# Running gate sums broadcast by DMA instead of transposed, GpSimd's rotation behind two additions, two attention steps moved, the last norm's weights on ScalarE

## What is computed

```python
# first layer: gated delta rule, 8 q/k heads, 16 value heads, chunks of 64 in the reference
g = -exp(a_log) * softplus(aa + dt_bias)
g = cumsum(g over the chunk)                        # running gate sums
diff = g[..., :, None] - g[..., None, :]
decay = exp(where(causal, diff, -inf))
a_strict = where(strict, beta[..., :, None] * kk * decay, 0)
sol = triangular_solve(a_strict, rhs, unit_diagonal=True)
qk = einsum(q, k) * decay
# beside it: 8 heads of dilated attention, with a rotation of the first 32 columns
q_b = partial_rope(bq, pos); k_b = partial_rope(bk, pos)
y = concatenate([y_a, y_b]) @ w_out
# ... other layers ...
return x * rsqrt(mean(x * x) + eps) * norm_final_g  # last norm
```

## Time and profile before

| | us |
|---|---|
| median of 3 runs | 2892.57 (2891.11 to 2893.55) |
| the profiled execution | 2890.94 |
| its span, first to last instruction | 2889.2 |

### The profile page before, as it was taken

One profiled execution on the slowest core, in us unless ns is written; L12 is line 12 of the kernel. 1 busy time (PEld: TensorE's weight loads), 2 busy tenths in 40 slices (PEclk: granted clock), 3 DMA queues, 4 the chain that ended last, 5 costly groups with the idle time before them and its releaser, 6 DMA issues.

```text
span 2889.2 us, 51927 instructions
## 1 busy us (share of the span) xinstructions
PE 2839.9 (98%) x17818; PEld 2521.2 (87%) x17818; DVE 2143.4 (74%) x3130; ACT 1484.7 (51%) x2140; POOL 452.5 (16%) x188
## 2 busy tenths in 40 slices
PE   7999999999999999999999999999999999999998
PEld 6888888888888888888897999988888888888887
DVE  7777777777679888888887899987786446565456
ACT  4454444444344444444445788865545444444443
POOL 0111101111000000000000000000004445455453
PEclk9999999999999999999999999999999999999999
DMA  6544444545568888788886777766775567667555
GB/s 235 170 151 150 160 157 158 165 162 174 162 211 306 308 298 314 281 318 305 302 287 209 221 239 238 231 207 236 282 286 175 194 214 242 230 232 251 199 183 181
DMA packets 211197, 651.81 MB, mean 226 GB/s; under 512 B 34552, under 2 KB 54392, under 8 KB 210304
## 3 DMA queue, kind: packets, MB, share of 16 engines
q1 hardware_dynamic: 177120, 616.61, 61.9%
q10 hardware_dynamic: 33952, 33.52, 3.7%
HBM read 626.95 MB, written 23.09 MB: 225 GB/s over the span
## 4 chain that ended last, share of the span: by engine, by line
PE 65%; issue 25%; DVE 5%; ACT 3%; DMA 1%; DVEq 0%; ACTq 0%; SPq 0%; POOL 0%; POOLq 0%
PE gemm L626 39%; PE gemm L630 20%; DVE wl L1697 2%; ACT wh L1101 1%; PE gemm L623 1%; PE gemm L624 1%; DVE dT L1895 1%; DVE dW L1893 1%; DMA raw<-in_stream 1%; DVE gB L1915 0%; ACT gA L1211 0%; DVE cb L1702 0%; ACT gB L1204 0%; PE side L761 0%; PE side L783 0%
## 5 line engine op out<-in xcount | busy, mean ns | idle before, releaser
L1101 ACT ACTIVATE wh<-raw 128x1024 fp32r<-128x1024 f32 x939 | 983.1, 1058 | 934.5 <-PE gemm L630 811.2
L626 PE MATMUL gemm<-xs,wh 128*128 128x512 f32 x4320 | 1363.7, 397 | 10.0 <-DVE cb L1702 3.4
L1697 DVE TENSOR_TENSOR wl<-raw,wh 128x1024 fp32r<-128x1024 f32 x811 | 1033.9, 1280 | 426.3 <-ACT wh L1101 404.5
L630 PEld LDWEIGHTS gemm<-xs,wl 128*128 128x128 f32 x5088 | 927.9, 188 | 180.7
L630 PE MATMUL gemm<-xs,wl 128*128 128x256 f32 x5088 | 1004.8, 279 | 0.0
L626 PEld LDWEIGHTS gemm<-xs,wh 128*128 128x128 f32 x4320 | 656.7, 188 | 21.4 <-DVE cb L1702 7.4
L626 PE MATMUL gemm<-hid,wh 128*128 128x512 f32 x2112 | 664.5, 396 | 4.7 <-DVE xacc L1717 2.3
L630 PEld LDWEIGHTS gemm<-hid,wl 128*128 128x128 f32 x2368 | 436.0, 188 | 90.4
L630 PE MATMUL gemm<-hid,wl 128*128 128x256 f32 x2368 | 467.3, 279 | 0.0
L1625 POOL TENSOR_TENSOR wl<-raw,wh 128x1024 fp32r<-128x1024 f32 x128 | 348.1, 2724 | 362.4 <-ACT wh L1101 361.1
L626 PEld LDWEIGHTS gemm<-hid,wh 128*128 128x128 f32 x2112 | 318.4, 188 | 7.4 <-issue 2.8
(11 more groups left out here) (416 smaller groups left out, 2132.0 us busy)
## 6 DMA issues: line engine op xcount, KB each, us to landing
raw<-in_stream SPq DMA_DIRECT2D x940, 512.0 KB, 4.2
ada_a<-in_ada SPq DMA_DIRECT2D x144, 512.0 KB, 5.0
ada_b<-in_ada SPq DMA_DIRECT2D x48, 512.0 KB, 4.9
parts_scratch<-parts SPq DMA_DIRECT2D x28, 256.0 KB, 4.0
pairs<-parts_scratch SPq DMA_DIRECT2D x112, 64.0 KB, 3.6
stash<-stage ACTq DMA_DIRECT2D x12, 512.0 KB, 4.5
att<-stash ACTq DMA_DIRECT2D x8, 384.0 KB, 5.2
x<-in_x SPq DMA_DIRECT2D x4, 512.0 KB, 5.7
```

What stands on the lines that cost most here:

```text
L626: mm(G[n][:, :], w, moving, start=first, stop=False, skip_group_check=True)
L630: op = mm(G[n][:, 0:T] if whole else G[n][:, T:2 * T], wl[:, slot, at:at + P], rhs(sl * SLAB_K + k)[:, 0:T], start=False, stop=last, skip_ ...
L1101: A(wh[:, slot, :], raw[:, slot, :], ACT.Copy).then_inc(hi_ready, 1)
L1697: tt(wl[:, slot, :], raw[:, slot, :], wh[:, slot, :].bitcast(F32), ALU.subtract).then_inc(lo_ready[slot], 1)
```

## The change

- The gate sums of all heads are transposed once (head 0, slot 43: TensorE; slot 44: VectorE), written to DRAM by ScalarE's queue (slot 45), and each head's four rows are read back, spread over 128 partitions, into `gbc` in SBUF, by one DMA of ScalarE's queue a head ahead. TensorE's four `gsel` transposes and GpSimd's copy go. VectorE's `gB` and `gA` additions read `gbc` in SBUF instead of PSUM, and so does ScalarE's `eg`.
- GpSimd's rotation waits for `d_gm`, which VectorE's `gA` addition sets.
- Attention steps 2 and 3 go from slots 9 and 12 to 12 and 17, on all engines.
- `into_x` takes each bank's two additions one after the other, instead of the first of two banks and then the second of both.
- In the last stage ScalarE multiplies x by the last norm's weights, in place, 12 of 16 tiles at early slots of the groups and four after the last squares; VectorE's 16 operations become 5 over 2, 3, 4, 4 and 3 tiles, with a DMA behind each.

```diff
+    gbc = nc.alloc_sbuf_tensor_at("gbc", [P, 4, P], F32, offset=hid_at + 15 * 2 * T * 4)
-    ATTN_AT = {1: 0, 6: 1, 9: 2, 12: 3, 33: 4, 37: 5, 40: 6, 43: 7}
+    ATTN_AT = {1: 0, 6: 1, 12: 2, 17: 3, 33: 4, 37: 5, 40: 6, 43: 7}
+    OUT_PARTS = [(0, 2), (2, 5), (5, 9), (9, 13), (13, 16)]
...
 # TensorE, delta step 1
-                    nc.tensor.transpose(ps0[:, j * P:(j + 1) * P], rn[:, j:j + 1].to_broadcast([P, P]), ident)
-                for j in range(4):
-                    op = nc.tensor.transpose(ps1[:, j * P:(j + 1) * P], gsel[:, j:j + 1].to_broadcast([P, P]), ident)
+                    op = nc.tensor.transpose(ps0[:, j * P:(j + 1) * P], rn[:, j:j + 1].to_broadcast([P, P]), ident)
...
 # ScalarE
+        def rows_of(it):
+            row = gates_dram[it:it + 1, :] if isinstance(it, int) else gates_dram[bass.ds(it, 1), :]
+            act.dma_start(gbc[:, :, :].rearrange("p a i -> p (a i)"), row.to_broadcast([P, 4 * P])).then_inc(gates_moved, 16)
...
+                if not isinstance(it, int) or it + 1 < QK_HEADS:
+                    act.wait_ge(S("a_eg"), it + 1)
+                    rows_of(it + 1)
...
+        def weights(i, j):
+            k = 4 * i + j
+            act.wait_ge(norm_sq, SQ_AT[4] + (i + 1 if i < 3 else 4 + j))
+            A(x[:, k, :], x[:, k, :], ACT.Copy, scale=V("final2", k, 1)).then_inc(weighted, 1)
...
 # GpSimd
-                    nc.gpsimd.tensor_copy(gsel[:, :], gcum[:, bass.ds(2 * it, 2), :])
...
                     pool.wait_ge(S("b_half"), it + 1)
+                    pool.wait_ge(S("d_gm"), it + 1)
                     nc.gpsimd.tensor_tensor(rb[:, :, :], rb[:, :, :], sinb, ALU.mult)
...
 # VectorE, into_x
                 summed(tmp[:, n, :], slice(0, T), n, base[:, 4 * i + n, :]).then_inc(tmp_ready, 1)
-            for n in two:
                 dve.wait_ge(tmp_ready, 4 * (g - whole_before) + n + 1)
                 summed(out[:, 4 * i + n, :], slice(T, 2 * T), n, tmp[:, n, :]).then_inc(bank_freed, 1)
...
 # VectorE, delta step 1
                 dve.wait_ge(S("p_bc"), it + 1)
-                pv = ps1[:, :].rearrange("p (j i) -> p j i", j=4)
+                dve.wait_ge(gates_moved, 16 * it + 64)
+                pv = gbc[:, :, :]
                 tt(gB[:, :, :], pv, four(H("mask_s")), ALU.add).then_inc(S("d_gB"), 1)
...
 # VectorE, the end
-        for q in range(4):
-            for j in range(4):
-                k = 4 * q + j
-                op = stt(x[:, k, :], x[:, k, :], V("final2", k, 1), ps1[:, 0:T], ALU.mult, ALU.mult)
-            op.then_inc(S("out_ready"), 1)
+        for k0, k1 in OUT_PARTS:
+            dve.wait_ge(weighted, LOADED + k1)
+            tt(x[:, k0:k1, :], x[:, k0:k1, :], ps1[:, 0:T].unsqueeze(1).to_broadcast([P, k1 - k0, T]), ALU.mult
+               ).then_inc(S("out_ready"), 1)
```

More of the change, by code:

```diff
@@ L197, in program @@
     qe = place("qe", [P, 2, P])
-    gsel = place("gsel", [P, 4])
     gcum = place("gcum", [P, V_HEADS, 2])
@@ L223, in program @@
     wab_at = nc.alloc_sbuf_tensor_at("wab", [P, KC, 32], F32, offset=gates_at + KC * P * 4)
+    grow = nc.alloc_sbuf_tensor_at("grow", [32, P], F32, offset=hid_at + 14 * 2 * T * 4)
+    gbc = nc.alloc_sbuf_tensor_at("gbc", [P, 4, P], F32, offset=hid_at + 15 * 2 * T * 4)
     gsum = nc.alloc_sbuf_tensor_at("gsum", [64, 2 * T], F32, offset=gates_at + KC * (P + 32) * 4)
@@ L326, in program @@
     parts_dram = nc.dram_tensor("parts_scratch", (4, P, 2 * T), F32).ap()
+    gates_dram = nc.dram_tensor("gates_scratch", (QK_HEADS, 4 * P), F32).ap()
     bias_dram = nc.dram_tensor("bias_scratch", (8, 512), F32).ap()
@@ L350, in program @@
     LOADED = 16
+    gates_moved = loads["hyb"]
+    weighted = loads["x0"]
     norm_sq, norm_acc, norm_sum, norm_var, norm_rn, norm_bc = (
@@ L430, in program @@
     TAP_AT = {19: 0, 22: 1, 25: 2, 28: 3}
-    GATE_PE, GATE_ACT = {24: 0, 31: 1, 39: 2}, {12: 0, 35: 1, 37: 2, 41: 3}
-    GATE_DVE = {14: 0, 27: 1, 34: 2, 36: 3, 38: 4, 40: 5, 42: 6}
+    GATE_PE, GATE_ACT = {24: 0, 31: 1, 39: 2, 43: 3}, {12: 0, 35: 1, 37: 2, 41: 3, 45: 4, 47: 5}
+    GATE_DVE = {14: 0, 27: 1, 34: 2, 36: 3, 38: 4, 40: 5, 42: 6, 44: 7}
     ATT_GROUPS = [(0, 8), (2, 4), (3, 4), (4, 8), (6, 4), (7, 4), (8, 4), (9, 4)]
@@ L575, in _ @@
             sp.wait_ge(raw_in[slot], 16 * (Q_END + 1))
[L576 to L579, removed]
+        for part, (k0, k1) in enumerate(OUT_PARTS):
+            sp.wait_ge(S("out_ready"), part + 1)
+            sp.dma_start(out_d[:, k0:k1, :], x[:, k0:k1, :]).then_inc(S("out_stored"), 16)
+        sp.wait_ge(S("out_stored"), 16 * len(OUT_PARTS))
     @block.tensor
@@ L724, in gates @@
                 op.then_inc(S("gate_pe"), 1)
+            elif step == 3:
+                pe.wait_ge(S("gate_dve"), 6)
+                nc.tensor.transpose(ps1[0:32, 0:P], gcum[:, :, :].rearrange("p h c -> p (h c)"), ident
+                                    ).then_inc(S("gate_pe"), 1)
         def delta(s, it):
@@ L1186, in gates @@
                 A(kdecf[:, :, :], kdecf[:, :, :], ACT.Exp).then_inc(S("gate_act"), 1)
+            elif step == 4:
+                act.wait_ge(S("gate_dve"), 7)
+                act.dma_start(gates_dram.rearrange("i (a p) -> (i a) p", p=P), grow[:, :]).then_inc(gates_moved, 16)
+            elif step == 5:
+                act.wait_ge(gates_moved, 48)
+                rows_of(0)
         def conv(slot, h):
@@ L1206, in delta @@
                 act.wait_ge(S("d_gm"), it + 1)
-                A(eg[:, :, :], ps1[:, :].rearrange("p (v c i) -> p v c i", v=2, c=2)[:, :, 1, :],
+                A(eg[:, :, :], gbc[:, :, :].rearrange("p (v c) i -> p v c i", c=2)[:, :, 1, :],
                   ACT.Exp).then_inc(S("a_eg"), 1)
@@ L1610, in _, with hook @@
             ff_in(FF_QUARTERS - 1, i)
+        def weights(i, j):
+            k = 4 * i + j
+            act.wait_ge(norm_sq, SQ_AT[4] + (i + 1 if i < 3 else 4 + j))
+            A(x[:, k, :], x[:, k, :], ACT.Copy, scale=V("final2", k, 1)).then_inc(weighted, 1)
         for i in range(4):
-            walk(Q_FF + 16 * (FF_QUARTERS - 1) + 8 + 2 * i, 8, split)
+            def hook(slot):
+                if i > 0 and slot in (1, 3, 5, 7):
+                    weights(i - 1, slot // 2)
+            walk(Q_FF + 16 * (FF_QUARTERS - 1) + 8 + 2 * i, 8, split, hook)
             squares(4, i)
+        for j in range(4):
+            weights(3, j)
     @block.gpsimd
@@ L1865, in gates @@
                 link(tt(bexp[:, :, :], bexp[:, :, :], beta[:, :, :], ALU.mult))
+            elif step == 7:
+                dve.wait_ge(S("gate_pe"), 4)
+                nc.vector.tensor_copy(grow[:, :], ps1[0:32, 0:P]).then_inc(S("gate_dve"), 1)
         def conv(slot, h):
```

## The result

| us | before | after |
|---|---|---|
| median of 6 runs | 2893.39 (2891.11 to 2897.65) | 2921.69 (2920.96 to 2923.9) |
| span of the profiled execution | 2889.2 | 2920.0 |
| mean granted TensorE clock | 0.998 | 0.992 |

The ratio is 1.0097, 95% interval 1.0087 to 1.0107: the change costs 28 us, 1%. The forecast was 2908 with a range to 2914. So the direction was right and the size too small by 14 us, almost half of the loss.

A forecast was written before the change was run, and what follows sets the result against it. It took VectorE's chain to slot 16 to set each head, making TensorE wait. About +2.1 us in each of eight heads (+17) less 1.6 at the last norm gave +15.4, so 2908 us, range 2890 to 2914.

The forecast's parts named there:

- `cb` later: lock less the moved `Sb`: VectorE's `cb` additions before slot 16: +2.0 us from the lock, -0.65 from the moved `Sb`, +1.35 per head.
- step 3's four matmuls behind slot 16: Attention step 3 on TensorE, formerly hidden in the wait before slot 16, moves to slot 17: +0.78 us per head.
- last norm: VectorE's final operations, 6.36 us before, take 4.7 to 5.0; gain 1.4 to 1.7, taken 1.6 us.
- Where the kernel is bound: Delta steps: TensorE late at slot 16 because VectorE's chain is late, losing 0.6 us in every head.
- The lock: GpSimd's held second rotation shuts out VectorE's split behind `gA`: about 3.2 instead of 1.23 us, ending 2.0 late per head.
- Attention steps: Steps 2 and 3 moved: `cb` 0.65 us earlier, L848's wait goes into slot 16's, step 3 adds 0.78.
- The stand itself: TensorE's wait for `cb` at slot 16 grows to some 3 us per head; summed as +2.1, eight times +17.
- gsel transposes, SBUF additions, ScalarE's DMA: Per-head gate work: each taken as 0; transposes up to 2.8 us gain, additions ±0.1 per head, DMA issue 0 to 0.4.
- The hold: GpSimd's rotation waiting for `d_gm` avoids the lock that `gB` and `gA` from SBUF would need; no separate size.
- B: Rival: VectorE's split not locked out, +0.13 us per head; 2892, no change; chance 0.19.
- C: Rival: slot 16's wait vanishes, TensorE alone sets the time, some 1.75 us gained per head; 2877; chance 0.11 with other gains.
- D: Rival: lock plus ScalarE's issue and slower additions, or solve-rotation collisions, 2.6 to 3 us per head; 2912 to 2916; chance 0.04.

The follow-up runs named there:

- e3: Changed kernel with three unused products more on TensorE at slot 15, filling its stand before slot 16; 2913.13 us, ratio 1.0070.
- e1: Kernel before with one line more: GpSimd's rotation waits for `d_gm`; 2910.12 us, ratio 1.0054.
- e5: Kernel before with only attention steps 2 and 3 moved to slots 12 and 17; 2895.87 us, ratio 1.0016.
- e6: Changed kernel with attention steps 2 and 3 back at slots 9 and 12; 2908.10 us, ratio 1.0056.
- e10: Changed kernel with e2's wait, e8's later solve, delta steps 10 to 16 one slot later, attention steps at slots 10 and 13; 2898.13 us, ratio 1.0016.
- e9: e8 with delta steps 10 to 16 one slot later, plus the change's last norm and order of additions; 2894.96 us, ratio 1.0004 to the kernel before.
- e4: Changed kernel without the hold, GpSimd's rotation no longer waiting for `d_gm`; 2927.86 us, ratio 1.0124 to the kernel before.
- e2: Changed kernel with GpSimd's second rotation waiting until VectorE's split of slot 4 is done; 2898.64 us, ratio 1.0018 to the kernel before.
- e7: Kernel before with only the change's last norm and `into_x` order of additions; 2891.99 us, ratio 0.9996.
- e11: Changed kernel unaltered, run once more for a second profile; one execution, 2924.94 us.
- e12: e8 with delta steps 10 to 22 two slots later; 2907.59 us, ratio 1.0049 to the kernel before.
- e8: Kernel before with three rows of VectorE's solve moved from slot 11 to 15 and attention step 3 to slot 13; 2890.57 us, ratio 0.9996.

## Why the prediction was wrong, by its steps

| term, us over eight passes unless said | forecast | measured |
|---|---|---|
| `cb` later: lock less the moved `Sb` | 10.8 | 12.6 (1.58 a pass) |
| step 3's four matmuls behind slot 16 | 6.2 | 7.0 (0.87 a pass) |
| clock behind the stands | not in the sum | 9.5 |
| slow transfers, last pass | not in the sum | 2.5 |
| start, and after the passes | 0 | 0.6 |
| last norm | -1.6 | -1.4 |
| **sum** | **15.4** | **30.8** (spans: 30.8) |

All are shifts of the same matmul against the kernel before. In the third pass of after the shift is 7.79 ahead of slot 2 and 9.34 at the first product of slot 16, so `cb` comes 1.55 later; the first seven passes have 1.5 to 1.9. The last has 4.07, 2.5 more than the pass before it. Step 3 is read in e3, where the clock stays full: from 7.17 to 8.04 in the third pass, 0.87. The 9.5 is the difference of after and e3 at the end of the passes (31.96 - 22.44). As the last pass of e3 still slowed, it is rather too small than too large. Without the clock and the last pass, a pass costs 2.45 against the 2.1 of the forecast.

- *Where the kernel is bound.* Right. TensorE is late where VectorE is late, and VectorE's chain from `gA` to `cb` sets each head.
- *The lock.* Right in mechanism, place and size: asked 0.24 behind GpSimd's start, 3.23 long where "about 3.2" was said; 2.38 for the first two rotations and 3.27 for the third. e1 shows it with one line. The shift of `cb` was 1.58 where 1.35 was said. The moved `Sb` gave 0.5 and not 0.65 (e5 alone has 0.5). And TensorE, late by a slab (the waits for `wl` in the list of after), frees a buffer later, so that VectorE's split of 295.89 waits 0.23 for L635.
- *Attention steps.* Right in kind. The wait at L848 went into the stand at slot 16, and step 3 came out behind it at 0.87 a head, not 0.78: the four matmuls take 0.68 from start to start (306.11 to 306.79), but the products just behind them are slower too. What the argument did not see is that it thereby **gathers three stands, one of 2.2 and two of up to 0.5, into one of 3.0** (e6 against after).
- *The stand itself: the step that failed.* The sum took a stand of some 3 us at its length: "Together +2.1, eight times +17 us". The forecast even named a wait of "some 3 us per head" and did not ask what a stand three times as long as the longest of the earlier trace rows does to TensorE afterwards. It costs 0.9 to 1.2 us more in seven passes and 2.4 in the seventh (after against e3), because the matmuls behind it run at 1.2 GHz for 3.4 us, or 6.8. With it the sum is 15.4 + 9.5 = 24.9, or 2917.
- *The last pass* was priced like the others. Its reload was not in any row that the forecast read, and its lateness could not have been told from them; it is the second term that the sum lacks, 2.5 us.
- *gsel transposes, SBUF additions, ScalarE's DMA.* Right at 0. e10 against e9 finds no gain even with the collision cured, though the two differ in more; `gB` and `gA` take 0.67; ScalarE's issue (0.37) lies beside the exponentials.
- *The hold.* "Which is what the hold avoids" was right: without it `gA` takes 2.21, and the kernel is 6 us slower (e4).
- *The end.* Right: 4.68 for the forecast's "4.7 to 5.0", 1.4 gained for 1.6.
- *The rivals.* B (the split is not locked out) is refuted by the row of 282.74; e2 shows what it would have given, 2898.64 and not 2892, since `cb` comes only 0.4 sooner, step 3 costs 0.87 and the clock falls in three passes. C would have needed the chain to slot 16 to come 2.2 us sooner; it came later. D named other causes, and none of them is there: the split asks 3.40 behind `gA`'s start and asked 3.36 behind it before, so ScalarE's issue costs 0.04; the additions are no slower; and the last rotation ends at 288.23, before VectorE's pair and the solve (290.80). The range ended at the sum's own bounds, and had nothing for a price outside the sum.

The parts timed alone give 16.5 (e1) + 2.9 (e5) - 1.0 (e7) = 18.4 of the whole's 28.3. The 10 that are missing are of the size of the clock and the last pass (9.5 and 2.5), which only the parts together bring about; the two sums agree to 2 us and no better.

## What to carry to other kernels

Price a wait of TensorE not by its length alone: where a change gathers short waits into one of about 3 us, look in the trace for places where it stood as long, and read the granted clock behind them. The price is a chance and not a certainty (see e4). Where GpSimd is held behind an event, follow its back-to-back operations forward in time to the next VectorE operation with both inputs in SBUF, and let them hand over by a semaphore (e2: 23 us from one wait). Before moving a step off the path, look for the next thing that waits for its result; in an order written by hand there was always one.

## What the runs showed of the hardware

- **The clock falls at stands that are short against the span, but not by their length alone.** Stands of 3.0 us and more at slot 16 came with the half clock each time in after and e11, and in four of five cases in e4, whose 3.33 was not. Where the longest of a pass was 1.6 to 2.3 (e1, e2, e6) it fell in three or four passes of eight, and at 1.1 (e3), 1.2 to 1.7 (e5), 1.45 (e12) and up to 1.8 (e8) in none. The slow stretch was 3.4 us long, or 6.8, and the pair of L631 and pair of L635 took 1.28 in it for 0.7. The kernel before has one outside the passes, from 850.86, behind sixteen one-column matmuls (L651, from 847.53) and a wait of only 0.27. What decides besides the length is not shown. The granted clock is full or half in every trace. The Trainium skill (TensorE: Matmul & The Clock Gate, Part 1) has these two states in its table, with the lower granted to an engine that has been idle. The traces agree with the two levels.
- **A mean clock of 0.992 for 0.998 is not small.** In the passes it was 34 us at half speed. Only 9.5 of them were lost (after against e3). In part TensorE stood anyway: the half clock of 749.1 begins 1.8 us before the stand ends.
- **Being 0.24 us late costs 2 us.** The loser of the lock waits for the whole instruction. But an operation that stands right behind another of its own engine is not always kept out: `gB` in e4.
- **A store of one matrix set took 5.1 to 5.4 us for 3.3 to 3.8**, in the last pass of after, e11 and e3. In its last 1.8 us the DMA engines were 4 to 5% busy. Its cause is open.
